# Where the gate blocks of a 16-head forget-attention layer are computed

## The reference, cut to what matters

```python
q, k, v, z, f_logit = jnp.split(h @ w_in, [FOX_AD, 2 * FOX_AD, 3 * FOX_AD, 4 * FOX_AD], axis=-1)
q = rms_norm(q.reshape(B, S, H, Dh), g_q).transpose(0, 2, 1, 3)     # H = 16 heads, Dh = 64
k = rms_norm(k.reshape(B, S, H, Dh), g_k).transpose(0, 2, 1, 3)
F = jnp.cumsum(jax.nn.log_sigmoid(f_logit + b_f), axis=1).transpose(0, 2, 1)
...
s = q k^T * scale + F[query] - F[key]; p = softmax(where(causal, s, -inf)); o = p @ v   # blocks of 128 queries
return (o * jax.nn.silu(z)) @ w_out
```

## Time and profile before

| | |
|---|---|
| median of 3 runs | 2964.33 us (2962.85 to 2973.53) |
| profiled execution | 2964.53 us, span 2962.4 us |
| PE busy | 2686.0 us (91%) |
| DVE busy | 1450.1 us (49%) |
| ACT busy | 1072.6 us (36%) |
| mean granted PE clock | 0.932 of full speed |
| share of PE in the chain that ended last | 77% (DVE 10%, ACT 8%) |

### The profile page before, as it was taken

How to read it: one execution, slowest core, us unless ns; L and a number is a source line. 1 busy time by engine, 2 the same in 40 slices (tenths; PEclk the granted TensorE clock), 3 DMA queues, 4 the chain that set the end, 5 groups by cost and what they waited for, 6 DMA issues and landing times.

```text
span 2962.4 us, 33229 instructions
## 1 busy us (share of the span) xinstructions
PE 2686.0 (91%) x13178; PEld 2148.9 (73%) x13178; DVE 1450.1 (49%) x2374; ACT 1072.6 (36%) x1873; POOL 268.9 (9%) x420
## 2 busy tenths in 40 slices
PE   6898999999889899999999999999778687899998
PEld 4677777787357677886578888888437676688887
DVE  5667566553574556521244333358345655443322
ACT  3445432522454454534333222242423333332221
POOL 5242121010000131000000000010000100000000
PEclk9899999999799999999599999999669888999999
DMA  5522273364002411421013333242100000133332
GB/s 208 174 72 86 90 259 113 114 208 135 29 30 73 135 30 57 132 65 43 29 44 100 100 95 97 80 121 87 49 0 1 1 1 1 57 100 93 100 93 78
DMA packets 146227, 250.16 MB, mean 84 GB/s; under 512 B 15455, under 2 KB 65914, under 8 KB 145049
## 3 DMA queue, kind: packets, MB, share of 16 engines
q1 hardware_dynamic: 129008, 198.08, 21.4%
q0 software_dynamic: 14816, 48.31, 4.9%
q10 hardware_dynamic: 2249, 1.65, 0.2%
HBM read 245.84 MB, written 5.30 MB: 85 GB/s over the span
## 4 chain that ended last, share of the span: by engine, by line
PE 77%; DVE 10%; ACT 8%; DMA 3%; issue 2%; POOL 0%; SPq 0%; DVEq 0%; ACTq 0%
PE PS L217 19%; PE PS L218 18%; PE PS L219 18%; PE PS L1743 2%; PE PS L984 2%; PE PS L1759 2%; ACT tmp L751 1%; PE PS L2309 1%; PE PS L1750 1%; PE PS L2312 1%; PE PS L2322 1%; DMA hT_b<-in_w_mod 1%; PE PS L2319 1%; DVE x L807 1%; PE PS L1444 1%
## 5 line engine op out<-in xcount | busy, mean ns | idle before, releaser
L209 DVE TENSOR_TENSOR w_lo<-w_raw,w_hi 128x1024 fp32r<-128x1024 f32 (+1 forms) x344 | 412.5, 1206 | 777.0 <-ACT w_hi L202 775.8
L202 ACT ACTIVATE w_hi<-w_raw 128x1024 fp32r<-128x1024 f32 (+1 forms) x344 | 356.4, 1045 | 1043.9 <-DMA w_raw<-in_ffn_w_gate_up 302.9
L217 PE MATMUL PS<-hT_hi,w_hi 128*128 128x512 f32 (+1 forms) x1728 | 665.3, 385 | 23.2 <-DVE hT_lo L819 13.8
L218 PE MATMUL PS<-hT_lo,w_hi 128*128 128x512 f32 (+1 forms) x1728 | 655.3, 379 | 0.0
L219 PE MATMUL PS<-hT_hi,w_lo 128*128 128x512 f32 (+1 forms) x1728 | 655.2, 379 | 0.0
L217 PEld LDWEIGHTS PS<-hT_hi,w_hi 128*128 128x128 f32 x1728 | 331.7, 192 | 89.7 <-issue 22.0
L219 PEld LDWEIGHTS PS<-hT_hi,w_lo 128*128 128x128 f32 x1728 | 332.3, 192 | 60.1
L218 PEld LDWEIGHTS PS<-hT_lo,w_hi 128*128 128x128 f32 x1728 | 332.7, 193 | 56.1 <-issue 0.2
L217 PE MATMUL PS<-w_hi,hT_hi 128*128 128x512 f32 (+1 forms) x704 | 289.6, 411 | 37.7 <-DVE hT_lo L2717 9.1
L218 PE MATMUL PS<-w_lo,hT_hi 128*128 128x512 f32 (+1 forms) x704 | 277.4, 394 | 0.0
L219 PE MATMUL PS<-w_hi,hT_lo 128*128 128x512 f32 (+1 forms) x704 | 276.8, 393 | 0.0
(11 more groups left out here) (546 smaller groups left out, 3625.9 us busy)
## 6 DMA issues: line engine op xcount, KB each, us to landing
w_raw<-in_ffn_w_gate_up SPq DMA_DIRECT2D x176, 256.0 KB, 3.1
mraw<-in_w_mod POOLq DMA_DIRECT2D x160, 256.0 KB, 4.0
w_raw<-in_gla_w_in SPq DMA_DIRECT2D x48, 512.0 KB, 4.7
w_raw<-in_ffn_w_down SPq DMA_DIRECT2D x44, 512.0 KB, 3.7
w_raw<-in_fox_w_in SPq DMA_DIRECT2D x32, 512.0 KB, 4.1
w_raw<-in_sgu_w_in SPq DMA_DIRECT2D x24, 512.0 KB, 5.1
w_raw<-in_dn_w_in SPq DMA_DIRECT2D x24, 512.0 KB, 3.6
w_raw<-in_gla_w_out SPq DMA_DIRECT2D x16, 512.0 KB, 4.8
```

What stands on the lines that cost most here:

```text
L202: nc.scalar.activation(w_hi[:, n % NS, :, 0:m], w_raw[:, n % NS, :, 0:m], ACT.Copy).then_inc(w_hidone, 1)
L209: nc.vector.tensor_tensor(w_lo[:, n % NS, :, 0:m], w_raw[:, n % NS, :, 0:m], w_hi[:, n % NS, :, 0:m].bitcast(F32), ALU.subtract).then_inc( ...
L217: nc.tensor.matmul(o, l_hi, r_hi, start=start, stop=False)
L218: nc.tensor.matmul(o, l_hi, r_lo, start=False, stop=False)
```

## The change

Z0 and Z1 are no longer projected as blocks of four banks. Each is made of four `fill`s, one tile of 128 output columns in one bank, over all eight steps (24 PE passes). The fills of Z0 stand in the norm stage: two before the spreads, two in portions between the spreads. Those of Z1 stand between units 8 and 42, one step (three passes) for each unit. The squares and their sums for 12 of the 16 tiles move into the V1 block, in another order of tiles; the small projection and F move up behind Q0; the F rows are moved by POOL's queue and not by SP's, and rows of heads 1 to 3 wait until all spreads are done, because the slots hold other data until then. Chunks that can only be loaded later are rounded at units 3, 5, 7, 9, 46, 48, 50 and 53. Z1 is copied out plain at units 17, 26, 35 and 44 and gets one `Silu` over all four tiles at unit 45. The gate is one DVE instruction; the split into the operand's two parts comes later, at units 47 to 59 and after the end. Another layer only takes over two semaphores.

```diff
+            NT_ = 2 * NP
+            NR = 2 * NT_
+            r = region(f"fox{j}", FR=([P, 4, S],), qT=([P, KT, S],), kT=([P, KT, S],), v=([P, TT, D],), szT=([P, KT, S],),
+                       cm=([P, P],),
                        mask=([P, P], BF16), unit=([P, P], BF16), sums=([P, 4 * FH],), gains=([P, 8],),
                        st=([P, 3, 4],))
+            rows_ = region(f"fox{j}s", pad=([P, S],), rlo=([NR, S], F32R), rhi=([NR, S], F32R))
+            r.rlo, r.rhi, r.rr = rows_.rlo, rows_.rhi, mraw[0:NR, 2, 0, :]
+            pick = region(f"fox{j}p", pad=([P, 4 * S + 28 * S],), pick=([NR, 4 * S], F32R)).pick
...
-            spread = hT_hi[0:2 * FH, 0:4, :].rearrange("p k s -> p (k s)")
-            nh = norm_heads(Group(sq=0, sum=0, root=0, rows=0, nrm=0), 2 * NP, 2, 4, (4, 7), r.sums,
-                            lambda n: Pb[:, n % 2, :], lambda n: (r.qT, r.kT)[n % 2][:, n // 2, :],
-                            lambda n: r.gains[:, n % 2:n % 2 + 1], (PT[:, 0, :], hT_hi[:, 7, :], hT_lo[:, 7, :]),
-                            lambda n: spread[:, P * n:P * (n + 1)])
+            sq_at = (hf[:, 0, :], hf[:, 1, :], ajunk[:], r.FR[:, 2, :])
+            tile = lambda n: (r.qT if n < NP else r.kT)[:, n % NP, :]
...
+            V0, Q0, Q1, K0, K1, V1, Z0, Z1 = wb
...
-            q.a_hi, q.a_lo, q.out_ready = hT_hi, hT_lo, None
+            q.a_hi, q.a_lo, q.out_ready = hT_hi, hT_lo, lambda c: (q.os, os_at + CK * c + CK)
...
+            Z_AT = {8 + 9 * n + s: (4 + n, s) for n in range(4) for s in range(KT)}
+            ZC_AT = {17 + 9 * n: 4 + n for n in range(4)}
+            FEED_AT = {3: Z1.first + 2, 5: Z1.first + 3, 7: ob.first, 9: ob.first + 1,
+                       46: ob.first + 2, 48: ob.first + 3, 50: ob.first + 4, 53: ob.first + 5}
+            OPER_AT = {47: 0, 49: 1, 51: 2, 54: 3, 56: 4, 59: 5}
+
+            def z_bank(n):
+                return (3, 7)[n % 2] if n < 4 else 7
...
-                for n in range(ob.first, ob.first + NS):
-                    sp_chunk(n)
-                sp.wait_ge(q.F_done, 1)
-                sp.dma_start(decay_rows[:, :], r.F).then_inc(q.flat, 16)
-                sp.wait_ge(q.flat, 16)
-                for h in range(FH):
-                    if h >= 4:
-                        sp.wait_ge(q.ttr, 2 * TT * (h // 2 - 1))
-                    sp.dma_start(r.FR[:, h % 4, :], bass.AP(decay_rows.tensor, h * S, [[0, P], [1, S]])).then_inc(FR_in[h % 4], 16)
-                for n in range(ob.first + NS, ob.last + 1):
+                for n in range(ob.first, ob.last + 1):
                     sp_chunk(n)
...
-                for n, b in list(zip(kinds, wb))[1:]:
-                    pe_block(b, tok_forms(b) if n == 5 else T_forms(b), hT_hi, hT_lo)
-                t_.wait_ge(ps_evac, wb[-1].ev)
+
+                def fill(n, s0, s1):
+                    b, m = (Z0, Z1)[n // 4], n % 4
+                    if s0 == 0 and n >= 2:
+                        t_.wait_ge(*z_taken(n - 1 if n >= 4 else n - 2))
+                    for s in range(s0, s1):
+                        c, k = s // CK, s % CK
+                        if m == 0 and k == 0:
+                            t_.wait_ge(w_lodone, b.first + c + 1)
+                        mm = form_pass(("T", z_bank(n), m * P), b.first + c, c, k, hT_hi, hT_lo, s == 0, s == KT - 1)
+                        if m == 3 and k == CK - 1:
+                            mm.then_inc(w_used, 1)
+                    if s1 == KT and m < 3:
...
+                def lengths(n0, n1):
+                    for n in range(n0, n1):
+                        t_.wait_ge(lens.sq, n + 1)
+                        t_.matmul(PS[0:NR, 0, :], r.sums[:, NR - 2 * n:2 * NR - 2 * n], sq_at[n % 4], start=n == 0,
+                                  stop=n == NT_ - 1).then_inc(lens.sum, 1)
+
+                def spread(n):
+                    if n >= 2:
+                        t_.wait_ge(lens.nrm, n - 1)
+                    sel = pick[:, n * P:(n + 1) * P]
+                    t_.matmul(PS[:, 1 + n % 2, :], sel, r.rhi[:], start=True, stop=False)
+                    t_.matmul(PS[:, 1 + n % 2, :], sel, r.rlo[:], start=False, stop=True).then_inc(lens.sum, 1)
+
...
+                pe_block(Q0, T_forms(Q0), hT_hi, hT_lo)
+                t_.wait_ge(ps_evac, V0.ev)
                 small_project(1, FH)
-                t_.wait_ge(q.bones, 1)
-                nh.pe()
+                t_.wait_ge(q.lz, 1)
+                for b in (Q1, K0, K1):
+                    pe_block(b, T_forms(b), hT_hi, hT_lo)
+                t_.wait_ge(ps_evac, K0.ev)
+                for c in range(V1.n):
+                    t_.wait_ge(w_lodone, V1.first + c + 1)
+                    for form in tok_forms(V1):
+                        for k in range(CK):
+                            mm = form_pass(form, V1.first + c, c, k, hT_hi, hT_lo, c == 0 and k == 0, c == V1.n - 1 and k == CK - 1)
+                    mm.then_inc(w_used, 1)
+                    if c == 0:
+                        t_.wait_ge(ps_evac, K1.ev)
+                        t_.wait_ge(q.bones, 1)
+                    if c < 3:
+                        lengths(4 * c, 4 * c + 4)
+                lengths(12, NT_)
+                fill(0, 0, KT)
+                t_.wait_ge(ps_evac, V1.ev)
+                fill(1, 0, KT)
+                t_.wait_ge(lens.rows, 1)
+                for n in range(NT_):
+                    spread(n)
+                    if n % 2:
+                        s = n - 1
+                        fill(2 + s // KT, s % KT, s % KT + 2)
                 t_.wait_ge(q.cmb, 1)
...
+                    if u == 0:
+                        t_.wait_ge(*z_taken(2))
...
-                            t_.wait_ge(q.os, os_at + h // 2 - 1)
+                            t_.wait_ge(q.gt, h // 2 - 1)
...
+                    for u2 in (u, u + 1):
+                        if u2 in Z_AT:
+                            n, s = Z_AT[u2]
+                            fill(n, s, s + 1)
                     if u < len(units):
                         turn(u)
                         turn(u + 1)
-                t_.wait_ge(q.os, os_at + KT)
+                t_.wait_ge(q.gt, NP)
...
-                for n, b in zip(kinds, wb):
+
+                def square(n):
+                    if n >= 4:
+                        a.wait_ge(lens.sum, n - 3)
+                    a.activation(sq_at[n % 4], tile(n), ACT.Square, scale=float(FD) ** -0.5).then_inc(lens.sq, 1)
+
+                for n, b in zip(kinds[:6], wb[:6]):
+                    if b is V1:
+                        a.wait_ge(ps_evac, K1.ev)
+                        for m in range(12):
+                            square(m)
+                            if m % 4 == 3:
+                                act_feed(V1.first + NS + m // 4)
...
-                    elif n < 6:
+                    else:
                         a.activation(r.v[:, :, (n - 4) * BW:(n - 3) * BW], src, ACT.Copy).then_inc(ps_evac, 1)
-                    else:
-                        a.activation(r.szT[:, 4 * (n - 6):4 * (n - 5), :], src, ACT.Silu).then_inc(ps_evac, 1)
-                a.wait_ge(ps_evac, wb[-1].ev)
+                    if b is Q0:
+                        a.wait_ge(small.mm, 2)
+                        a.wait_ge(q.cols, 80)
+                        a.activation(r.F, PS[0:FH, 1, :], ACT.Identity, bias=r.gains[0:FH, 2:3]).then_inc(q.lz, 1)
+                        a.wait_ge(q.lz, 1)
+                        z = r.FR[0:FH, 0, :]
+                        then_act(a.activation(z, r.F, ACT.Abs))
+                        then_act(a.activation(z, z, ACT.Exp, scale=-1.0))
+                        a.activation(z, z, ACT.Ln, bias=1.0).then_inc(q.lz, 1)
+                for m in range(12, NT_):
+                    square(m)
+                act_feed(Z1.first + 1)
+                a.wait_ge(lens.sum, NT_)
...
+                a.activation(r.rr, PS[0:NR, 0, :], ACT.Sqrt, bias=eps[0:NR]).then_inc(lens.root, 1)
+
+                def z_take(n):
+                    a.wait_ge(*z_made(n))
+                    a.activation(r.szT[:, n, :], PS[:, z_bank(n), :], ACT.Silu if n < 4 else ACT.Copy).then_inc(
+                        ps_evac if n % 4 == 3 else q.ze, 1)
+
+                for n in range(4):
+                    z_take(n)
...
+                    if u in ZC_AT:
+                        z_take(ZC_AT[u])
...
+                    if u in FEED_AT:
+                        act_feed(FEED_AT[u])
+                    if u == 45:
+                        a.wait_ge(*z_taken(7))
+                        a.activation(r.szT[:, 4:8, :], r.szT[:, 4:8, :], ACT.Silu).then_inc(q.f1, 1)
...
-                pool_mod(i + 1)
...
+                pool_mod(i + 1, after_two=masks)
+                p.wait_ge(q.F_done, 1)
+                p.dma_start(decay_rows[:, :], r.F).then_inc(q.flat, 16)
+                p.wait_ge(q.flat, 16)
+                for h in range(FH):
+                    if h == 1:
```

(70 more changed lines are left out.)

46 lines of the change are left out of this document (23 added, 23 removed).

## The result

The changed kernel takes 2991.34 us (median of 6, 2984.95 to 3001.14) against 2968.93 for the kernel before (6 runs, 2961.95 to 2976.56): ratio 1.0081, 95% interval 1.0051 to 1.011. It is slower by 0.8%, 1.3 us above the range. The profiled execution took 2990.8 us, its span is 2989.0 against 2962.4, so 26.6 us more.

The account below looks back on a forecast made before the run. Norm stage bound by a serial chain with PE idle or slow, units by a ring through all three engines. 48.9 us lost less 42.9 gained gave +6.0 on 2964.5: 2970.5 us, range 2947 to 2990.

Parts of the forecast that it names:

- fills: Units: Z1's 96 passes in 18 groups, partly covering PE's wait for DVE; +20.9 us, bounds +14 and +27.
- `Silu`: Unit 45: two table loads and the activation delay the values; +4.4 us, bounds +2 and +7.
- operand splits: Units 47 to 59: 1.16 us each on DVE, nearly bare at odd units behind a chunk; +4.3 us, bounds +1 and +7.
- row of head 1: First units: F row on POOL's queue lands after it is needed; +1.8 us.
- gate, out wait, copies, clock at the start: Units and output projection: gate -1.0, shorter out wait -1.1, Z1 copies +1.2, first units no longer at 1.2 GHz -1.3 us.
- chunks, with what they do to the clock: Units 3, 5, 7, 9, 46, 48, 50, 53: rounding in strictly ordered queues delays PE; +19.7 us, bounds +8 and +26.
- 0.6, the slack of the next two units: Units with chunks: 0.6 us taken off the stall of each of the eight chunks.
- The clock rival: Units 3 to 9: PE's clock falls and stays 1.2 GHz through the fills; +21 us, 2990 us; chance 0.16.
- under 5, since PE isn't the bound there: Units 45 to 53: a clock fall there alone costs under 5 us.
- 1 us for changes between kinds of passes: Norm stage: 1 us allowed for changes between kinds of passes within the 30.7 us before the first score.
- The rival of a norm stage that isn't hidden: Norm stage: spreads at half clock or late rows give back 8 of 21.3 us gained; 2978.5 us; chance 0.07.
- The cheap rival: Units: each chunk costs 1.04 us and fills cover all of PE's pause; 2952 us, 2949.5 with cheap `Silu`; chance 0.22.

Follow-up runs that it names:

- e4_tinyfill: Changed kernel with the 32 fill steps of Z1 cut to one matmul of 16 columns each: stage 147.9 us against 163.9, median 2978.47 us, ratio 1.0016.
- e11_lagtinyfill: Changed kernel with VectorE's chunk rounding two units later and Z1's 32 fill steps cut to one small matmul each: stage 119.5 us, median 2950.87 us, ratio 0.993.
- e2_nosilu: Changed kernel with the one Silu over four gate blocks at unit 45 replaced by a one-column copy: stage 160.1 us, median 2990.87 us, ratio 1.0065.
- e13_latesplit: Changed kernel with VectorE's chunk rounding two units later and all operand splits after the last gate: stage 134.4 us, median 2964.95 us, ratio 0.9985.
- e1_lag: Changed kernel with VectorE rounding each chunk two units after ScalarE rounds its half: stage 135.6 us against 163.9, median 2966.95 us, ratio 0.9985.
- e7_lagrows2: Changed kernel with VectorE's chunk rounding two units later and decay rows of heads 0 and 1 loaded early: stage 131.6 us, median 2965.7 us, ratio 0.9985.
- e3_rows2: Changed kernel with decay rows of heads 0 and 1 loaded ahead of the units: stage 166.2 us against 163.9, median 2995.46 us, ratio 1.0084.
- e12_z0group4: Changed kernel with Z0 as a four-bank block, Z1 filled in the norm stage, spreads and fills grouped by four: stage 96.2 us, median 2946.82 us, ratio 0.9917.
- e9_group4: Changed kernel with VectorE's chunk rounding two units later and spreads and fills alternating in fours: stage 135.2 us, median 2962.51 us, ratio 0.9977.

## Why the prediction was wrong, by its own steps

I had given "the same" a chance of 0.58 and "slower", above 2979.1 us, one of 0.25; slower came. The direction of each part was right: the norm stage gained, the units lost. The sum missed 16.3 us in the units and 6.7 ahead of them, and the rest of the program gave 2.4 back.

| term | forecast | measured | from |
|---|---|---|---|
| fills | 20.9 | 16 | e4_tinyfill, e11_lagtinyfill |
| `Silu` | 4.4 | 3.7 (4.7 up to the next chunk) | e2_nosilu |
| operand splits | 4.3 | 2 to 5.5 | e13_latesplit against e1_lag and e7_lagrows2 |
| row of head 1 | 1.8 | 0 beside the chunk waits, 0.3 to 2.3 without them | e3_rows2, e7_lagrows2, e13_latesplit |
| gate, out wait, copies, clock at the start | -2.2 | not measured | |
| chunks, with what they do to the clock | 19.7 | 39 to 46 | what remains of 65.2; 28.3 of it went with the lag |

**The chunks: this step failed.** Their mechanism was the one described (ScalarE can round only behind evac(u-1), VectorE waits, ttr and scale come behind), and TensorE's idle times came as worked out: 3.62, 3.92, 3.70 and 3.31 us at units 3, 5, 7 and 9 and 3.92 at 53 where 3.8 was said, and 1.77, 1.47 and 2.43 at the three even units where 2.7, 1.5 and 2.0 were. Together 24.1 us, 24.5 in the prediction. Two things were mis-sized. I took off "0.6, the slack of the next two units" from each, 4.8 in all; nothing in the traces shows it. And I priced the stalls at the clock of the earlier trace rows. TensorE's work between them ran mostly at 1.2 GHz at both ends of the units: 10.3 us by the busy time of the same 769 matmuls in the lagged kernel, 6 to 9 by the added matmuls. With 24 of idle time that makes 30 to 34 of the 39 to 46; where the other 5 to 16 us lie stays open.

**The clock rival had the right place and the wrong extent.** It said that the clock falls at the waits of units 3 to 9 and then stays down through the fills. It fell there, but the fills brought it back: 1.00 from 800 to 858. And it fell among the last chunks too, at units 46 to 53 and some units behind them (0.61 in 866 to 896), where I had written that this costs "under 5, since PE isn't the bound there". TensorE is not the busiest engine there (19.15 us, VectorE 19.52), but its scores and transposes are links of the serial chain that each chunk hangs on (754.54 to 757.71 in the chain above), so their length counts. The rule on bursts parted by waits (the Trainium skill, TensorE: Matmul & The Clock Gate, HAM oscillation — how this bites in real kernels) agrees with the two ends; by the row of 800 to 858 it doesn't reach steps of six matmuls between waits of under a microsecond. That this rival's 2990 us is near the result is chance: its 21 us for slow fills didn't occur.

**Fills, `Silu`, splits, row.** The fills were 4.9 us too dear in the sum, at most: the small matmuls in their place aren't free. The `Silu` was right to within 1 us. The splits can't be told from right by these runs. The row's 1.8 lies inside what it cost with the lag, but beside the chunk at unit 3 it cost nothing.

**Ahead of the units.** First score at 748.7 and not 742. The spread phase holds 2.6 of the 6.7 us: I gave "1 us for changes between kinds of passes", and there are 16 at 0.2. The squares hold some 2: the wait of 2.6 was right, but the clock dropped in it (0.95 in 700 to 712), and the last eight sums took 5.1 us (710.9 to 716.0) instead of the 3.6 of a group before. Another 1.3 was there before the change could act: the passes behind the layer's first wait for a rounded chunk start at 562.95 and not at 561.70. The rest, under 1 us, is less than what the first score differs by from run to run of the same code (746.1 to 751.1). The rival of a norm stage that isn't hidden was wrong in its cause: the spreads ran at 1.00 throughout.

**The cheap rival** (2952) came near for the fills alone (it had 14 us for them, e4_tinyfill has 16). Its queue that runs far enough ahead is what e1_lag builds by hand.

Of my three signs of being wrong, a first score later than 748 came true, by 0.7 us; units under 130 us did not (163 from the first score to the last gate, where I had about 146), and VectorE rounded no chunk while TensorE still had work behind it at units 3 to 9. The last is the sign that the mechanism was right, and only its price wrong.

## What to carry to other kernels

Where work that two engines do one after the other is put into a ring of strictly ordered queues, put the second half later in its queue than the first half can possibly end; the wait costs more than both halves' work (28 us against 18 for eight chunks here), and moving one line recovers it: e1_lag takes the same time as the kernel before to 0.15%. Price such a stall with the clock that TensorE has beside it, and count TensorE's work there in full if the stalled chain runs through it. A piece that can be placed among passes that leave room on the other engines is cheaper there than in a ring that has little: the same projection of Z0 and Z1 outside the units made this kernel 0.7 to 0.8% faster than before instead of 0.8% slower.

## What the runs showed that I had not expected

The clock came back during the fills: 0.50 in 774 to 782 of the changed kernel, 0.95 from 782 to 786, 1.00 from 800, with waits still between the steps. And after a wait of 2.48 us between two full stretches it can fall for the next four sums (3.48 us for four) or not (1.90 us in e12_z0group4 behind the same 2.48 us), so the same code differs by 1.6 us there from one execution to the next.

The same holds for the last units. With the lag, the stretch from the fifth gate to the last took 34.19 and 34.20 us at 0.83 in two executions and 30.55 us at 0.95 in a third (e1_lag, e9_group4, e7_lagrows2), with the same instructions there. A difference of 4 us in the stage of two single profiles says nothing about an edit before one has looked where it arises.
